# Rotation of q and k: the mean of squares as two F32R products over a high and a low part, the low part made by GpSimd

## The reference, cut to what matters

```python
def rms_norm(x, g):
    xf = x.astype(jnp.float32)
    y = xf * lax.rsqrt(jnp.mean(xf * xf, axis=-1, keepdims=True) + NORM_EPS)
    return (y * g.astype(jnp.float32)).astype(x.dtype)
...
        z = h @ w_in[l]
        q = z[..., :o1].reshape(B, S, N_Q_HEADS, HEAD_DIM)
        k = z[..., o1:o2].reshape(B, S, N_KV_HEADS, HEAD_DIM)
...
        q = apply_rope(rms_norm(q, q_norm_g[l]), cos, sin)
        k = apply_rope(rms_norm(k, k_norm_g[l]), cos, sin)
```

## Time and profile before

| | us |
|---|---|
| median of 3 runs | 3350.57 |
| the 3 runs | 3344.0, 3350.57, 3350.88 |
| the profiled execution's own time | 3348.95 |
| its span, first to last instruction | 3347.1 |
| PE busy (share of the span) | 3152.6 (94%) |
| DVE busy | 2410.5 (72%) |
| ACT busy | 1265.8 (38%) |
| POOL busy | 195.0 (6%) |

### The profile page before, as it was taken

The page is one execution under the profiler, slowest core; times in us unless marked ns, Lnnn a source line. Parts: engine busy times, 40 slices in busy tenths (PEclk is TensorE's granted clock), DMA queues, the critical chain, the costliest instruction groups (busy, mean ns, idle before and its releaser), DMA issues.

```text
span 3347.1 us, 35342 instructions
## 1 busy us (share of the span) xinstructions
PE 3152.6 (94%) x13945; PEld 2538.3 (76%) x13945; DVE 2410.5 (72%) x2655; ACT 1265.8 (38%) x1650; POOL 195.0 (6%) x287
## 2 busy tenths in 40 slices
PE   4899999997899999959999999999999899999997
PEld 4677777775788888847878888888888788888885
DVE  5559687774499999956665567767767677776767
ACT  4423111111699999923333432222223221212122
POOL 0001522441000000000000000000000000000000
PEclk8899999998999999979999999999999999999999
DMA  7633422223611112056766521121125311111113
GB/s 278 197 143 135 139 107 80 85 85 142 182 41 36 35 32 54 17 163 192 238 214 221 190 75 54 49 62 54 50 62 181 109 45 49 54 42 61 41 62 121
DMA packets 137973, 349.29 MB, mean 104 GB/s; under 512 B 26664, under 2 KB 35752, under 8 KB 133320
## 3 DMA queue, kind: packets, MB, share of 16 engines
q1 hardware_dynamic: 120208, 302.98, 28.6%
q10 hardware_dynamic: 12096, 25.17, 2.0%
q0 software_dynamic: 5504, 18.88, 1.5%
HBM read 249.55 MB, written 92.19 MB: 102 GB/s over the span
## 4 chain that ended last, share of the span: by engine, by line
PE 49%; DVE 3%; DMA 3%; ACT 1%; issue 0%; SPq 0%; ACTq 0%; DVEq 0%
PE second_ps_a L90 10%; PE second_ps_a L91 10%; PE second_ps_a L92 10%; PE second_ps_b L90 6%; PE second_ps_b L91 6%; PE second_ps_b L92 6%; DMA merge_w_st<-in_w_branch 2%; DVE second_y L2144 1%; DMA merge_x<-scratch_rec 0%; DVE second_y L2162 0%; DVE second_y L2159 0%; ACT merge_wb_hi L1670 0%; DVE merge_wb_lo L1726 0%; DMA ffn_x<-scratch_x 0%; SPq L1612 0%
## 5 line engine op out<-in xcount | busy, mean ns | idle before, releaser
L2144 DVE TENSOR_TENSOR second_y<-second_y,second_ps_b 128x512 f32<-128x512 f32 x654 | 444.3, 687 | 206.2 <-PE second_ps_b L92 206.2
L90 PE MATMUL second_ps_a<-second_h_hi,up_wu_hi 128*128 128x512 f32 x1408 | 549.4, 390 | 4.4 <-DVE up_wu_lo L1893 4.3
L91 PE MATMUL second_ps_a<-second_h_lo,up_wu_hi 128*128 128x512 f32 x1408 | 549.1, 390 | 0.0
L92 PE MATMUL second_ps_a<-second_h_hi,up_wu_lo 128*128 128x512 f32 x1408 | 549.0, 390 | 0.0
L1284 DVE TENSOR_TENSOR att_prob_lo<-att_prob,att_prob_hi 128x1024 fp32r<-128x1024 f32 x256 | 309.7, 1220 | 26.3 <-ACT att_prob_hi L1250 25.3
L90 PEld LDWEIGHTS second_ps_a<-second_h_hi,up_wu_hi 128*128 128x128 f32 x1408 | 265.1, 188 | 60.6 <-DVE up_wu_lo L1893 5.5
L92 PEld LDWEIGHTS second_ps_a<-second_h_hi,up_wu_lo 128*128 128x128 f32 x1408 | 265.0, 188 | 55.2
L91 PEld LDWEIGHTS second_ps_a<-second_h_lo,up_wu_hi 128*128 128x128 f32 x1408 | 265.0, 188 | 55.0
L90 PE MATMUL proj_ps<-h_hi,proj_w_hi 128*128 128x512 f32 x704 | 293.3, 417 | 5.5 <-DVE proj_w_lo L811 5.5
L90 PE MATMUL second_ps_b<-ffn_wd_hi,ffn_g_hi 128*128 128x512 f32 x704 | 276.5, 393 | 19.9 <-ACT second_y L2062 11.2
L91 PE MATMUL second_ps_b<-ffn_wd_lo,ffn_g_hi 128*128 128x512 f32 x704 | 275.4, 391 | 0.0
(11 more groups left out here) (239 smaller groups left out, 5812.2 us busy)
## 6 DMA issues: line engine op xcount, KB each, us to landing
up_w_st<-in_w_up SPq DMA_DIRECT2D x88, 512.0 KB, 6.0
ffn_wd_st<-in_w_dn SPq DMA_DIRECT2D x44, 512.0 KB, 3.6
first_w_ada<-in_w_ada SPq DMA_DIRECT2D x32, 512.0 KB, 4.5
scratch_gates<-proj_out SPq DMA_DIRECT2D x64, 256.0 KB, 2.0
merge_w_st<-in_w_branch SPq DMA_DIRECT2D x32, 512.0 KB, 6.6
merge_gate<-scratch_gates SPq DMA_DIRECT2D x64, 256.0 KB, 3.1
scratch_h<-merge_x ACTq DMA_DIRECT2D x48, 256.0 KB, 5.1
first_raw_lo<-in_w_ada SPq DMA_DIRECT2D x8, 1024.0 KB, 13.2
```

Source lines behind the costliest of these rows:

```text
L90: pe.matmul(out, w_hi, x_hi, start=first, stop=False)
L91: pe.matmul(out, w_hi, x_lo, start=False, stop=False)
L92: return pe.matmul(out, w_lo, x_hi, start=False, stop=last)
L2144: dve.tensor_tensor(at, at, ps_d[:, q % 4, :], ALU.add).then_inc(s_y, 1)
```

## The change

The product of `sq` and `head_mean` becomes two accumulating F32R products: one with the high part of the squares, one with the low part, both with an F32R copy of `head_mean`. ACT makes the high part with a second `Square` of the same PSUM tile into `sq_hi` (its memory is `v_hl`, free at that time). POOL makes the low part, `sq - sq_hi`, in place of `sq`. PE now waits for POOL's `s_sql`. POOL's stores of a rotation are moved: in its stream those of rotation i-3 stand behind the subtraction of rotation i. The copy of `head_mean` (its memory is `mrow`) is one small DVE instruction at the start.

```diff
--- before.py
+++ after.py
@@ -539,12 +539,15 @@
         zg, sq, std, rot = (side[:, a, b * 2 * BLK:(b + 1) * 2 * BLK].rearrange("p (s q) -> p s q", s=2)
                             for a in (2, 3) for b in (0, 1))
         z, eo = (side[:, a, :].rearrange("p (n c) -> p n c", n=N1) for a in range(2))
+        sq_lo = nc.alloc_sbuf_tensor_at("proj_sq_lo", [P, 2, BLK], F32R, offset=side_at + (2 * S + 2 * BLK) * 4)
+        sq_hi, mean_r = v_hl, mrow
         k_hi = hi_st[:].rearrange("p n c -> p (n c)")
         ps_a, ps_b = (r.ps(f"ps{i}", [P, 2, BLK]) for i in range(2))
         ps_ms = r.ps("ps_ms", [P, 2, BLK])
         ps_sw = r.ps("ps_sw", [P, 2, BLK])
         ps_m = [ps_ms, ps_sw, ps_b]
         ps = [ps_a[:, 0, :], ps_a[:, 1, :], ps_b[:, 0, :], ps_b[:, 1, :]]
+        s_sql, s_mean = r.sem("squares_lo"), r.sem("mean_rounded")
         s_c, s_rt, s_eps = r.sem("consts"), r.sem("rotation_tables"), r.sem("eps_written")
         s_w = [r.sem(f"w_loaded{i}") for i in range(2)]
         s_hi, s_lo, s_mm, s_zg, s_ms, s_std, s_rot, s_out, s_rope = (
@@ -642,13 +645,21 @@
 
             @block.gpsimd
             def _(pool):
-                for c in range(NQC + 1):
-                    for n in range(NB):
-                        cols = slice(n * BLK, (n + 1) * BLK)
-                        pool.wait_ge(s_rhi, NB * c + n + 1)
-                        pool.dma_start(qk_d[0, c, :, cols], hi_st[:, n, :].bitcast(F32)).then_inc(s_st[n], 16)
-                        pool.wait_ge(s_rlo, NB * c + n + 1)
-                        pool.dma_start(qk_d[1, c, :, cols], out[:, n, :]).then_inc(s_st[n], 16)
+                def store_rotated(i):
+                    c, n = divmod(i, NB)
+                    cols = slice(n * BLK, (n + 1) * BLK)
+                    pool.wait_ge(s_rhi, i + 1)
+                    pool.dma_start(qk_d[0, c, :, cols], hi_st[:, n, :].bitcast(F32)).then_inc(s_st[n], 16)
+                    pool.wait_ge(s_rlo, i + 1)
+                    pool.dma_start(qk_d[1, c, :, cols], out[:, n, :]).then_inc(s_st[n], 16)
+
+                for i in range(NROPE):
+                    pool.wait_ge(s_zg, i + 1)
+                    pool.tensor_tensor(sq_lo[:, i % 2, :], sq[:, i % 2, :], sq_hi[:, i % 2, :], ALU.subtract).then_inc(s_sql, 1)
+                    if i >= 3:
+                        store_rotated(i - 3)
+                for i in range(NROPE - 3, NROPE):
+                    store_rotated(i)
                 n = 0
 
                 def step(ins):
@@ -774,7 +785,8 @@
                         if c or n >= 2:
                             act.wait_ge(s_rot, 4 * c + n - 1)
                         act.activation(zg[:, n % 2, :], ps[n], ACT.Copy, scale=gains[:, c:c + 1])
-                        act.activation(sq[:, n % 2, :], ps[n], ACT.Square).then_inc(s_zg, 1)
+                        act.activation(sq[:, n % 2, :], ps[n], ACT.Square)
+                        act.activation(sq_hi[:, n % 2, :], ps[n], ACT.Square).then_inc(s_zg, 1)
                         if c or n >= 2:
                             rotated_hi(4 * c + n - 2)
                         if n:
@@ -817,6 +829,8 @@
 
                 dve.memset(eps[:], EPS).then_inc(s_eps, 1)
                 lo_part(0, 0)
+                dve.wait_ge(s_c, 16 * 3)
+                dve.tensor_copy(mean_r[:], head_mean).then_inc(s_mean, 1)
                 dve.wait_ge(s_rt, 16 * 2)
                 for c in range(NQC + 1):
                     lo_part(c + 1, (c + 1) % 2)
@@ -892,11 +906,12 @@
 
                 def rope_products(c, n):
                     if c == 0 and n == 0:
-                        pe.wait_ge(s_c, 16 * 3)
-                    pe.wait_ge(s_zg, 4 * c + n + 1)
+                        pe.wait_ge(s_mean, 1)
+                    pe.wait_ge(s_sql, 4 * c + n + 1)
                     if c or n >= 2:
                         pe.wait_ge(s_rot, 4 * c + n - 1)
-                    pe.matmul(ps_ms[:, n % 2, :], head_mean, sq[:, n % 2, :], start=True, stop=True).then_inc(s_ms, 1)
+                    pe.matmul(ps_ms[:, n % 2, :], mean_r[:], sq_hi[:, n % 2, :], start=True, stop=False)
+                    pe.matmul(ps_ms[:, n % 2, :], mean_r[:], sq_lo[:, n % 2, :], start=False, stop=True).then_inc(s_ms, 1)
 
                 for c in range(NQC + 2):
                     pe.wait_ge(s_lo, c + 1)
```

## The result

| | us |
|---|---|
| before, median of 19 runs | 3346.81 |
| changed kernel, median of 19 runs | 3358.33 |
| ratio, 95% interval | 1.0031 (1.0024 to 1.0038) |

The changed kernel is 0.31% slower, some 10.4 us by the ratio. The forecast was 9.7 us slower, about 3360 us in all. That total started from the median of three runs of before, 3350.57; over 19 runs it is 3.8 lower.

A forecast was written before the change was run, and what follows sets the result against it. It took the rotations to be bound by a loop of multiply, copy, square, high part, root and reciprocal. 4.44 + 3.9 + 1.81 - 0.49 = +9.7 us on 3350.57 gave about 3360 us, range 3353 to 3367.

The forecast's parts named there:

- The product: On PE: two F32R matmuls replace the float32 product; only the last product's saving counts, -0.49 us.
- The second square: On ACT: it delays root and reciprocal by 0.48 us, nine times plus 0.12, +4.44 us.
- POOL ahead of the last product: At rotation 19: second square and POOL's subtraction start PE's last product 1.81 us later, counted once.
- POOL and DVE where n = 0: In chunks 1 to 4: POOL's subtraction holds up DVE's L832, 0.98 us each, 3.9 us in all.
- What costs nothing: In the rotations: POOL's moved stores, the small DVE copy of `head_mean` and DVE's later end stay covered.
- The sum: PE's last product comes 9.7 us later, giving a time of about 3360 us.
- DVE isn't held: Rival, where n = 0: POOL doesn't delay DVE; +5.8 us, 3356 us; chance 0.20.
- reciprocals are held too: Rival, where n = 3: POOL also blocks reciprocals, or is slow; up to +14.3 us, 3365 us; chance 0.12.
- PE sets the pace: Rival, in the rotations: the loop has slack and PE runs each turn 0.41 faster; -8.2 us, 3342 us; chance 0.07.
- absorbed: Rival, behind the rotations: a later PE wait takes up the delay; time stays 3350 to 3352 us; chance 0.07.
- PE's clock falls: Rival, in the rotations: PE's gaps drop it to 1.2 GHz, 4.9 us per turn, up to +73 us; chance 0.04.

The follow-up runs named there:

- e3: Kernel before with the mean taken of the squares' high part alone: one F32R product, one ACT square, nothing new on POOL; 3347.28 us, ratio 0.9996.
- e1: Kernel before with ACT's second square alone, written to free memory and read by nobody; float32 product, nothing on POOL; 3353.43 us, ratio 1.0016.
- e2: Changed kernel with POOL's subtraction also waiting for DVE's sum of the previous rotation, so the two never meet; 3354.52 us, ratio 1.0020 to before.
- e6: e5 with POOL waiting as in e2 and also making the finished rotation's low part in place of DVE; 3338.26 us, ratio 0.9975 to before.
- e7: e6 without the change under study: float32 squares and product, early root and POOL's low part of the rotation kept; 3343.03 us, ratio 0.9986.
- e5: Changed kernel with ACT's root of each rotation moved up into its own turn; 3348.95 us, ratio 1.0004 to before.

## Why the prediction was right

The direction, the size and the mechanism held. Step by step:

- *The product, -0.49.* The last mean product to the first product of the maxima took 376.0 - 334.26 = 41.7 us before and 384.2 - 342.92 = 41.3 after: -0.4 to -0.5. Where PE doesn't wait, the turn fell from 6.31 to 5.95, by 0.36 where the prediction has 0.41. That PE only waits more for the rest is shown by e3. One reading was off, without a price: PE doesn't yet follow the loop from rotation 4 on. Before, its products 0 to 9 stand 6.31 apart, and its first listed wait is at product 11 (279.10). Until then PE takes its own turns, the squares being ready ahead of it, and it doesn't hold the loop either, as e3's M shows.
- *The second square, +4.44, and 0.48 on the last product.* e1 has both together: D grew by 4.77 against 4.92 forecast. M holds seven of the ten delays, and it grew by 3.44, or 7 times 0.49.
- *POOL ahead of the last product.* Of the 1.81 forecast, 0.48 is the square's and 1.33 POOL's. The product came 3.90 - 2.04 = 1.86 later relative to the multiply of rotation 17. In e1, where it starts 336.51 - 333.98 = 2.53 after it, POOL is not there, so POOL's share is 3.90 - 2.53 = 1.37. D of e2 minus D of e1, 1.58, is that plus the 0.22 by which e2's product comes later still.
- *POOL and DVE where n = 0, 4 times 0.98 = 3.9.* In rotation 8 POOL ends 268.32 - 264.16 = 4.16 us after the multiply, where the prediction has 4.17. The four sums took about 0.96 longer each, and e2 took 3.84 of M away. The Trainium skill's rule (SBUF — State Buffer, section Who interferes with whom) agrees with these rows. Its part on instructions with one SBUF input, which the page gives only for those outside the two-port modes, agrees with the reciprocals beside POOL, which the trace of before doesn't have: 3.35 us at 267.86 in e6.
- *What costs nothing.* M is 100.55 in e1 and 100.54 in e2, and e2 has the moved stores and the copy of `head_mean` besides: neither holds the loop.
- *The sum.* D grew by 9.97 against 4.44 + 3.9 + 1.81 = 10.15, and to the last product of the maxima PE lost 9.5 us against 9.7. The ratio gives 10.4 with an interval of 8 to 13.

Of the rivals, "DVE isn't held" is out by the 1.66 us rows, "reciprocals are held too" by the reciprocals at 3.35, "PE sets the pace" by e3, and "absorbed" by the ratio. "PE's clock falls" did happen in part, without the price that I gave it; this is below. Two details were off. For PE's waits I said about 20 us that name POOL; they are 16.0, and ten of fourteen name nobody. In the two chunks in which the clock fell they sum to 3.5 us each, against 4.9 in the chunk ahead of them (products 6 to 9), which is 2.8 of what is missing. And POOL's subtractions took 1.64 where they met DVE, not 2.

## What to carry to other kernels

Before shortening an instruction, find the loop that sets the pace: some 12 us of TensorE work could be taken out here for nothing, while 0.48 us in the wrong place of ACT's stream was paid ten times over, 4.8 us in all. If a helper's result is needed a whole turn later, put what is on the loop (here the root) ahead of it. Give GpSimd its two-input work where VectorE runs a one-input instruction, with a semaphore that keeps them apart; then the split product pays, and e6 (0.25% below before) is the best version found.

## What was not expected

In the changed kernel PE waits 2.04 to 2.06 us four times, for the subtractions that follow the turns with n = 0 (products 6, 10, 14 and 18). Behind two of these waits the clock fell to the 1.2 GHz level. PE's timeline, and the windows around it (the last numbers are clock, DMA share and GB/s):

```profile
276.63 0.53 PE L913 MATMUL proj_ps_ms<-proj_v_hl,proj_mrow 128*128 128x512 f32 x1 [2.04 <-POOL proj_sq_lo L658]
276.96 0.63 PE L914 MATMUL proj_ps_ms<-proj_sq_lo,proj_mrow 128*128 128x512 f32 x1
```

```profile
276.00:280.00 4.00, 3.37 (x9) 2.69 (x10) 3.84 (x3) 0.12 (x1) 1.41 (x3) 0.61 0.52 197
...
308.00:312.00 4.00, 4.00 (x13) 3.10 (x12) 3.96 (x6) 1.73 (x4) 0.00 (x0) 0.62 0.17 62
```

The mean of 0.61 holds a stretch at the low level: from 277 to 280 us the clock was 0.50. The block behind took 7.63 us (product 276.63 to the next at 284.26) in place of 5.95, and the next product then started without a wait, 0.4 us later than where the clock stayed up (247.10 to 254.33, 7.23 us). One block later that was made up: from product 10 to product 12 it took 14.62 us, from product 6 to product 8 14.61, and the chunks follow each other 29.5 us apart with and without the fall. So PE's waits paid for the 1.7 us, and the end was not moved. In the windows 215 to 270 and 270 to 325 of e1 to e7 the clock was 1.00, e5 included, where PE's waits in those turns were also up to 2.1 us. Why it fell behind two waits and not behind the others stays open. The rival had the right rule, that only what exceeds the turn counts (4.9 us), but for whole turns at the low level; here each fall lasted some 3 to 4 us and cost 1.7, less than the waits of that chunk.
